# Weighting a second row by a diagonal matrix on TensorE, and loading the last norm's gain later, in the tail of a fused encoder kernel

## The reference

```python
def hier_moe(h, w_group, w_router, w_gate, w_up, w_down):
    """Top-1 expert group, then top-2 experts inside it; gated-MLP experts."""
    ...
    weights = g_w * top_p / jnp.sum(top_p, axis=-1, keepdims=True)
    ...
    hid = jax.nn.silu(a) * u * gates[:, :, None].astype(t.dtype)
    y = jnp.einsum('tef,efd->td', hid, w_down)
    return y.reshape(b, l, d)

    ...
        h = h + hier_moe(rms_norm(h, moe_norm[i]), moe_w_group[i], moe_w_router[i],
                         moe_w_gate[i], moe_w_up[i], moe_w_down[i])

    return rms_norm(h, final_norm)[:, CHUNK:]
```

## Time and profile before

| | |
|---|---|
| median of 3 runs | 1138.62 us (1138.2 to 1141.27) |
| the profiled execution's own time | 1140.07 us |
| its span, first to last instruction | 1138.4 us |
| busy: TensorE, VectorE, ScalarE, GpSimd | 92%, 39%, 23%, 21% |
| mean granted TensorE clock | 0.972 |
| chain that ended last, by engine | PE 79%, DVE 12%, issue 3%, DMA 2%, ACT 2%, POOL 1% |

### The profile page before, as it was taken

The page is one execution under the profiler, slowest core; times in us unless marked ns, Lnnn a source line. Parts: engine busy times, 40 slices in busy tenths (PEclk is TensorE's granted clock), DMA queues, the critical chain, the costliest instruction groups (busy, mean ns, idle before and its releaser), DMA issues.

```text
span 1138.4 us, 16440 instructions
## 1 busy us (share of the span) xinstructions
PE 1050.2 (92%) x6553; PEld 662.3 (58%) x6553; DVE 446.1 (39%) x806; ACT 263.5 (23%) x528; POOL 240.5 (21%) x232
## 2 busy tenths in 40 slices
PE   4999999999999999978999998989998978999982
PEld 4989979989988877753333332454444443333321
DVE  6400314224226540155132226557547745232216
ACT  5132143134224411020011111314214510111111
POOL 5333314205214533003000005510000002000004
PEclk9999999999999999988999998989999998999997
DMA  7232223114115121367899887030004058998945
GB/s 305 74 130 75 75 90 114 56 42 161 56 37 168 37 74 74 148 278 285 313 358 376 353 361 259 42 148 0 1 1 148 1 233 339 333 380 323 403 189 222
DMA packets 34838, 201.01 MB, mean 177 GB/s; under 512 B 4352, under 2 KB 4352, under 8 KB 25808
## 3 DMA queue, kind: packets, MB, share of 16 engines
q1 hardware_dynamic: 21168, 151.26, 34.7%
q10 hardware_dynamic: 8864, 31.74, 7.9%
q0 software_dynamic: 4736, 17.04, 4.1%
HBM read 303.70 MB, written 28.44 MB: 292 GB/s over the span
## 4 chain that ended last, share of the span: by engine, by line
PE 79%; DVE 12%; issue 3%; DMA 2%; ACT 2%; POOL 1%; SPq 0%; POOLq 0%; DVEq 0%; ACTq 0%
PE ps L844 30%; PE ps L1083 15%; PE ps L1102 7%; PE ps L969 4%; PE ps L1207 4%; PE ps L1149 3%; PE ps L850 3%; DVE arena L2079 2%; PE ps L1071 2%; DVE arena L2076 2%; PE ps L1060 1%; PE ps L912 1%; ACT arena L1522 1%; PE ps L1167 1%; DMA ring<-in_w_ret 1%
## 5 line engine op out<-in xcount | busy, mean ns | idle before, releaser
L844 PE MATMUL ps<-x_hi,ring_r 128*128 128x264 f32 x1024 | 190.9, 287 | 3.2 <-DVE xT L1562 3.1
L2159 POOL TENSOR_TENSOR ring_r<-ring,ring_r 128x1024 fp32r<-128x1024 f32 x56 | 136.9, 2459 | 260.5 <-ACT ring_r L1299 260.4
L844 PEld LDWEIGHTS ps<-x_hi,ring_r 128*128 128x128 f32 x1024 | 160.3, 190 | 3.6 <-issue 3.3
L1083 PE MATMUL ps<-arena,xT 128*32 128x512 f32 x864 | 158.0, 600 | 0.0
L1083 PE MATMUL ps<-ring,xT 128*32 128x512 f32 x672 | 143.9, 602 | 5.9 <-DVE xT L1562 5.9
L844 PE MATMUL ps<-xT_r,ring_r 128*128 128x264 f32 x512 | 146.2, 286 | 0.0
L1562 DVE TENSOR_TENSOR xT<-ps,gains 128x512 f32<-128x512 f32 (+1 forms) x76 | 46.9, 660 | 182.8 <-PE ps L1071 177.3
L844 PE MATMUL ps<-ring_r,x_hi 128*128 128x512 f32 x320 | 100.6, 395 | 0.0
L844 PEld LDWEIGHTS ps<-xT_r,ring_r 128*128 128x128 f32 x512 | 97.0, 189 | 0.1
L1102 PE MATMUL ps<-arena 128*32 128x512 f32 x624 | 87.3, 595 | 4.3 <-ACT arena L1436 4.3
L1299 ACT ACTIVATE ring_r<-ring 128x1024 fp32r<-128x1024 f32 x56 | 57.9, 1054 | 118.4 <-PE ps L844 70.8
(11 more groups left out here) (265 smaller groups left out, 1554.7 us busy)
## 6 DMA issues: line engine op xcount, KB each, us to landing
arena<-in_w_gu SPq DMA_DIRECT2D x22, 2048.0 KB, 14.8
ring<-in_w_gu SPq DMA_DIRECT2D x20, 2048.0 KB
arena<-in_w_down SPq DMA_DIRECT2D x36, 1024.0 KB
arena<-in_w_gu POOLq DMA_DIRECT2D x18, 2048.0 KB
ring<-in_w_gu POOLq DMA_DIRECT2D x14, 2048.0 KB
arena<-in_w_down POOLq DMA_DIRECT2D x26, 1024.0 KB
ring<-in_w_ret SPq DMA_DIRECT2D x48, 512.0 KB, 3.7
ring<-in_w_ret_out SPq DMA_DIRECT2D x16, 512.0 KB, 4.9
```

The lines of the kernel that those rows point to most:

```text
L844: last = mm(dst, a_parts[x], b_parts[y], start=(start and n == 0), stop=(stop and n == 2))
L1083: last = mm(ps[cols, b, :], xgT[:, k % 2, c, cols], by_row(gu(j))[:, c, :], start=(c == 0), stop=(c == KT - 1))
L2159: G.tensor_tensor(w_lo[slot][:, m], w_raw[slot][:, m], w_hi[to][:, m], ALU.subtract).then_inc(lo_made, 1)
```

## The change

In layer 1's tail the second choice's rows no longer go through VectorE. TensorE multiplies them by a diagonal matrix and accumulates onto the late product in the same PSUM banks, and `add_late` then adds both at once.

- ScalarE makes the four diagonals in expert round 8 of layer 1: identity matrix times the token's weight, 128x128 each (`diagonal`, raised by `diag_made`). They lie over `late_hot` and `late_second`, which are out of use by then.
- TensorE's `late_results` of layer 1 leaves its accumulation open; behind all four, `second_choices(t)` waits for the tile's gathers and the diagonals and adds two products of 128x512.
- VectorE does `first_choice(t)`, then `add_late(t)`, tile by tile. `second_choice` is gone in layer 1 (layer 0 keeps it), and `final_norm(0)` stands behind tile 2's `add_late` instead of ahead of tile 2's choices.
- ScalarE's squares wait for `add_late(t)` to have read the bank, instead of for `second_choice`.
- SyncE issues the gain's load only when tile 1's two gathers have landed. VectorE's wait for that load is where it was, ahead of its first tail instruction.

```diff
             for j in range(2):
                 sp.wait_ge(mo[1][f"y_out{j}"], results_stored(ROUNDS - 2 - j))
+            sp.wait_ge(mo[1]["gathered1"], 32)
             sp.dma_start(fin_g, a["final_norm"].partition_broadcast(128)).then_inc(fin_in, 16)
...
-                    last = mm(ps[0:r, b + c, :], late_w[:, at], yo[:, 1, 512 * c:512 * c + 512], start=True, stop=True)
+                    last = mm(ps[0:r, b + c, :], late_w[:, at], yo[:, 1, 512 * c:512 * c + 512], start=True, stop=(l == 0))
+                if l == 0:
+                    last.then_inc(full[b], 1)
+
+            def second_choices(t):
+
+                b = fl.bank(f"LC1_{t}")
+                pe.wait_ge(mo[1][f"gathered{t}"], 32)
+                pe.wait_ge(diag_made, NT)
+                for c in range(2):
+                    last = mm(ps[:, b + c, :], diagonal[:, t, :], gat[t][:, 1, 512 * c:512 * c + 512], start=False, stop=True)
                 last.then_inc(full[b], 1)
...
             for t in TILES5[1:]:
                 late_results(1, t)
+            for t in TILES5[1:]:
+                second_choices(t)
...
+                    if l and k == 8:
+                        act.wait_ge(m["gather_ready"], 1)
+                        for t in range(NT):
+                            nc.scalar.activation(diagonal[:, t, :], ident, ACT.Copy, scale=view(WE, 2, 5)[:, 1, t:t + 1])\
+                                .then_inc(diag_made, 1)
...
-            squares(MOE_TILES[1], nrm["_f"], next_junk, lambda t: act.wait_ge(mo[1]["gath_used"], t + 1))
+            squares(MOE_TILES[1], nrm["_f"], next_junk, lambda t: fl.wait_read(act, f"LC1_{t}"))
...
                     dve.wait_ge(m[f"gathered{t}"], 32)
-                    fl.wait_read(dve, f"LC{l}_{t}")
+                    if l == 0:
+                        fl.wait_read(dve, f"LC{l}_{t}")
                     step.done(weighted(t, 0))
...
-            add_late(0)
             for t in range(NT):
                 first_choice(t)
-                second_choice(t)
-                if t + 1 < NT:
-                    add_late(t + 1)
-                if t == 1:
+                last_step.wait()
+                add_late(t)
+                if t == 2:
                     final_norm(0)
             for t in range(1, NT):
                 final_norm(t)
```

More of the change, by code:

```diff
@@ L510, in build @@
         wo_b_in = sem("w_o_b_in")
-        fin_done, s_out, fin_in = sem("final_done"), sem("out_stored"), sem("final_gain_in")
+        fin_done, s_out, fin_in, diag_made = sem("final_done"), sem("out_stored"), sem("final_gain_in"), sem("diagonals_made")
         dsem = {k: sem(f"dve_steps_{k}") for k in ("retention", "attention")}
@@ L601, in build @@
         late_second = view(CMP + 256, 128)
+        diagonal = view(CMP, 4, 128)
         assert ends[-1] <= SMALL - 100, ends[-1]
@@ L1956, in add_late @@
                     V_.tensor_tensor(h[0:r, t, :], flat(ps[0:r, b:b + 2, :]), h[0:r, t, :], ALU.add).then_inc(free[b], 1)
-                return add_late, first_choice, second_choice
-            add_late, first_choice, second_choice = experts(0)
+                return add_late, first_choice, second_choice, step
+            add_late, first_choice, second_choice, _ = experts(0)
             step = Steps(dve, dsem["attention"])
@@ L2115, in _ @@
                     add_projection(t)
-            add_late, first_choice, second_choice = experts(1)
+            add_late, first_choice, _, last_step = experts(1)
             dve.wait_ge(fin_in, 16)
```

## The result

| | before | changed |
|---|---|---|
| median | 1138.41 us, 6 runs (1137.3 to 1141.57) | 1144.47 us, 6 runs (1143.66 to 1145.65) |
| profiled execution's own time, span | 1140.07, 1138.4 | 1143.66, 1141.9 |
| ratio, 95% interval | | 1.0047 (1.0034 to 1.006) |

By the ratio the changed kernel is slower by 0.47%, some 5.4 us (3.9 to 6.8 by the interval); the two medians are 6.1 us apart. The time lies above the forecast's range.

The account below looks back on a forecast made before the run. VectorE's start, held by the gain's load, and its work from there were taken to set the end: 1122.2 + 11.2 + 7.45 = 1140.85 for a span of 1138.4, +2.4 us, so 1141.0 us, range 1138.8 to 1143.6.

Parts of the forecast that it names:

- VectorE's work from the first weighted row on: VectorE's tail in layer 1: 11.2 us of gapless work, for 15.17 before, 4.0 us less.
- a start that nothing but TensorE holds: Rival: the gain doesn't hold VectorE's start, tile 0's sum runs at 1119.1; 2.0 us faster, 1136.6 us, chance 0.04.
- The work behind the last sum: End of the span: squares, root, norm and store after VectorE's last addition, unchanged at 7.45 us.
- The wait for the gain decides the start: VectorE's first tail instruction waits for the gain, starting at 1122.2 (1119.7 to 1123.5) instead of 1115.78, 6.4 us lost.
- The landing of tile 1's gathers: Tile 1's last gather, issued at 1111.5, takes 6.1 us and lands at 1117.6, between 1115.8 and 1118.3.
- The gain's load: SyncE's 512 KB load, issued behind tile 1's gathers, takes 4.5 us to land, between 3.8 and 5.1.
- The bound of 1.3 us for sharing with the gathers: Gain's load: 512 KB at 395 GB/s; even sharing with gathers adds up to 1.3 us to 3.8.
- The far row of 8.7 us: Layer 0's last bias load, also a 512 KB broadcast, behind four loads on its queue; kept out of the forecast.
- TensorE's products cost nothing: Second choices on TensorE, 7.1 us in all, hidden by 4.4 us at tile 0 and 5 us at tile 3.
- ScalarE's diagonals cost nothing: Round 8: four copies, 1.1 us, delay the last load of rows to 1085.1; TensorE needs it at 1087.21, 2.1 us cover.
- Served behind all gathers: Rival: the gain's load lands after the last gather plus 1.3 us, VectorE starts at 1124.7; 1143.5 us, chance 0.11.
- The sign of being wrong: VectorE's first weighted row (L1959) starting before 1119.7 or after 1123.5 would show the forecast wrong.

Follow-up runs that it names:

- the two ways of removing it: Changed kernel with VectorE's wait moved to its first final norm: ratio to before 0.9988; or with the gain's load issued ahead of the gathers: 0.9986.
- the second profile of the same tail: Profile of the kernel before with the four diagonals made on ScalarE in round 8 and not used: 1138.99 us, ratio 1.0, tail 27.7 us.
- behind tile 0: Changed kernel with the gain's load issued behind tile 0's gathers instead of tile 1's: 1141.07 us, ratio to before 1.002.

## Why the prediction was wrong

The mechanism was right and its price too small: slower by 2.4 us was forecast, by about 5.4 was measured, and the range ended at 1143.6 where 1144.47 came out. By its own steps:

- *VectorE's work from the first weighted row on*: 11.2 us forecast, 1123.33 to 1134.44 = 11.1 measured. Right, and so is the 4.0 us less than before: with the wait out of the way the tail lost 2.2 us against the profiled before, 2.0 forecast for a start that nothing but TensorE holds. The work behind the last sum took 7.46, for 7.45.
- *The wait for the gain decides the start*: right. 14.91 us of idle time on it, and each of the two ways of removing it turns the loss into a small gain.
- *The landing of tile 1's gathers*: 1110.50 + 6.29 = 1116.8, or 8.1 us after A, where the forecast had 1117.6 - 1109.96 = 7.6. The 6.1 us taken from layer 0 measured 6.3, and the gather was issued a little later against A. Half a microsecond too early.
- *The gain's load*: **the step that failed**. Forecast 4.5, at most 5.1; measured 6.44. The bound of 1.3 us for sharing with the gathers supposed that both queues move side by side from the first moment. They don't: 3.5 us pass with three packets of the load against 374 of the gathers' (the DMA rows above), where 1.0 us passes with nothing ahead. The far row of 8.7 us was in the profile and was set aside because nothing stood ahead on the same queue; what stands ahead on the other queues counts as well. That is 1.9 us.
- *The time before it is compared with*: its profiled execution had its first weighted row 5.8 us after A, the second profile of the same tail 5.2. The forecast's difference was taken from the slower of the two, some 0.7 us.

Together 2.4 + 0.5 + 1.9 + 0.7 = 5.5, against 5.4 measured (3.9 to 6.8 by the interval). The last 0.7 rests on a single second profile and is the least certain of these, though the ratios of the experiments fit a tail of 27.7 us better than one of 28.4.

- *TensorE's products cost nothing*: right, with 8 us to spare for the last. *ScalarE's diagonals cost nothing*: right, though for another reason than the cover of 2.1 us, since the load of rows behind them wasn't delayed at all.
- *The rivals.* "Served behind all gathers" gave 1143.5, nearest to the measured time, but its mechanism is only part of what happened: the load did wait until some 370 of the 461 outstanding packets had moved, and yet behind tile 0 it landed 3 us ahead of the last gather and 0.7 us ahead of one issued before it. In the changed kernel the load and the last gather landed within 0.3 us of each other, so that case alone couldn't have told them apart.
- *The chances.* 0.73 stood on a change within 0.3%, with a forecast of +2.4 us against a border of 3.4. One microsecond more on the gain's load, the one term without a near row, was enough to cross it.
- *The sign of being wrong.* A first weighted row after 1123.5 was to show the forecast wrong, and it came at 1123.33. That it passed is luck: this execution reached A 1.3 us earlier than the profiled one of before. Measured from A the bound was 13.5 us, and the row came at 14.65.

## What to carry to other kernels

When a load is moved later, look for the wait on it and ask what else stands behind that wait on its engine; a wait that cost nothing becomes the start of everything, and it belongs on the instruction that reads the data. Price a load that is issued into another queue's traffic by what is in flight at its issue, not by its size over the bandwidth: here 3.6 us became 5.7 with two gathers in flight, 6.4 with four, and 7.2 with four and two more to come. And compare tails, and set the signs of a forecast, from a common event inside the trace: that event came at times 4 us apart, while two profiles of the same tail were 0.7 us apart.

## What the runs showed of the hardware that was not expected

- A load of 512 KB on SyncE's queue, issued while GpSimd's gathers were in flight, moved 3 packets in its first 3.5 us against 374 of the gathers', and then went side by side with them. With none in flight its first packets moved after 1.0 us.
- ScalarE's DMA issue did not wait for the four operations ahead of it: the load of rows was issued at 1069.42, while the first diagonal ran from 1069.31 and the last three until 1070.6. In the kernel with the diagonals alone the two starts are as far apart, 1068.80 and 1068.91.
- TensorE kept the full clock (1.00) from 1117 to 1126 with a pause of 1.81 us in front of the last product; before, with no work from 1117.06 on, the same windows had 1.00 and then 0.53.
